# Two-layer decoder step: reordered loads, stores and waits at four seams, one test around the overflow loop, last-stage gathers two tiles ahead

## The chip, the core and the metric

The kernel runs on one core of one Trainium2 chip, as one launch. The metric is the device time of the launch in microseconds (us). Five engines run their own instruction streams and meet at semaphores: PE (matrix multiplication; its weight loads are listed as PEld), DVE (vector), ACT (activation functions; it also issues DMAs), POOL (indirect DMAs, the gathers) and SP (only issues DMAs and waits). A DMA issued by an engine stands in that engine's queue; the packets of all queues run on the same 16 DMA engines of the core.

## The reference

One step of a two-layer decoder on 1024 prompt rows and 8 sample rows, all in float32, width 1024. Each layer projects its input, runs three groups of heads (a gated convolution, latent attention, an mLSTM), multiplies with `w_out`, and sends each row to two of 32 experts. Cut to what bears on the change:

```python
def hybrid_layer(x, p, pos, ...):
    z = jnp.einsum('bld,dn->bln', x, w_in)
    q = jnp.einsum('blr,rn->bln', rms_norm(c_q, q_norm_g), w_uq)...
    ckv = rms_norm(c_kv, kv_norm_g)
    att = mla_prompt_attention(q_nope, q_rope, k_nope, krope, v)
    h_m, C1, n1, m1 = mlstm_chunkwise(...)
    y = rms_norm(jnp.concatenate([y_conv, y_mla, y_mlstm], -1)..., mix_norm_g)
    h1 = layer_norm(DN_ALPHA * x + jnp.einsum('blm,md->bld', y, w_out), ln1_g, ln1_b)
    moe = hier_moe(h1, ...)
    ple = jnp.einsum('blp,pd->bld', p, w_pe) * jax.nn.sigmoid(jnp.einsum('bld,de->ble', h1, w_pg))
    out = layer_norm(DN_ALPHA * h1 + moe + ple, ln2_g, ln2_b)
    return out, ckv, krope, conv_state, C1, n1, m1
```

## The kernel before

**Tiles and stages.** The rows are nine tiles: eight of 128 prompt rows (`TP` = 8) and a last one with the 8 sample rows (`LAST` = `TP`, `NT` = 9). A layer is four stages: `stream_project_prepare` (projections, mLSTM, queries, keys, values), prompt attention, sample attention, and `mix_route_experts` (`w_out`, routing, the gates `sigmoid(h1 @ w_pg)`, the experts). After layer 1 `combine_last` adds the expert rows to the base and normalises. Each engine's instructions of a stage are written out by hand in one function; waits are semaphore counts, so an engine that waits holds up all that stands behind it on that engine. Between stages every engine waits at a barrier (L114, one for each run of semaphores). The expert stage's loads follow a planned list of due times per expert.

**Projection to attention.** On SP, round `t` of the projection stores what tile `t-1` gave: latents (L408, L409), KT, V, QT (L433), then Y, the mLSTM output (L438, behind `y_ready`); in the round `t == LAST` the samples' Z follows (L441). The round `t == NT` loads the first pair of heads for attention (`first_qk`, L218 and L219, four loads of 96x1024; `first_v`, L227) and stores the sample tile's latents and its QT (96x8x8). SP then waits at L449 for the QT stores, which ends the stage on SP. The attention's first matmul is L1149.

**Gates.** `EARLY` lists the tiles whose gates are made before the experts start; the sample tile is number 4 of them. For number `i` ACT takes the sigmoid of PE's product (L2474, L2487 for the samples) into `sig[i % 2]`, copies a transposed p tile out of PSUM for PE (`p_copied`, L2459, which also issues the load of a later p tile, L2429), and stores the finished base rows of number `i-1` (`stored_base`, L2470). `sig` has two buffers, so from `i` = 2 on a wait for the store of number `i-2` stands ahead. The p tiles alternate between early and deferred ones (`P_ORDER`); deferred gates are made between the expert quads. PE transposes p (L2187) and multiplies it with `w_pe` (L2130, L2236).

**Overflow loop.** 21 quads of experts run with fixed capacity. Rows that don't fit go to at most 32 further blocks; their count `used` is read on the device and SP, PE, ACT and DVE each run `rest_turns` over them. Here `used` is 0.

**Last stage.** SP loads nine `base` tiles and the rows `g`, `b` of 128x1024; POOL gathers two expert rows per token into `r1`, `r2` (two indirect DMAs a tile, L2945); PE adds, for each tile, `ident @ base` (L2956) and `diag(weight) @ r` (L2960) in one PSUM tile; ACT builds the 18 diagonals (L3007); DVE and ACT normalise, SP stores the output.

## Time and profile before

| | |
|---|---|
| device time, median of 3 runs | 2455.68 us (2449.44 to 2460.41) |
| the profiled execution | 2454.07 us, of which the span of its instructions is 2452.3 us |
| PE busy | 2246.9 us, 92% of the span |
| DVE, ACT, POOL busy | 1160.3, 729.4, 335.6 us |
| HBM traffic | 382.90 MB read, 126.32 MB written, 208 GB/s over the span |

### The profile page before, as it was taken

The page shows a single profiled execution, that of the slowest core. Times are in us where ns is not written, and L with a number is a line of the kernel's source. Part 1 is how long each engine was busy: PE and PEld are TensorE (multiplying, and loading weights), DVE is VectorE, ACT ScalarE, POOL GpSimd, SP SyncE. Part 2 cuts the span into 40 slices and gives each one's busy share as a digit, 9 for nine tenths or more (in the row PEclk, how much of TensorE's full clock was granted, in tenths as well). Part 3 has the DMA queues.
Part 4 walks back from the last instruction along what each step waited for, and adds up shares of the span by engine and source line. Part 5 has one row for each costly group of instructions (what it writes and reads, how often), then busy time and mean ns, then how long its engine had stood idle before and what let it go on. Part 6 is the DMA issues. An engine that isn't in the chain of part 4 may idle for free. (4 is left out here: it accounts for less than half of the span.)

```text
span 2452.3 us, 39565 instructions
## 1 busy us (share of the span) xinstructions
PE 2246.9 (92%) x14448; PEld 1164.2 (47%) x14448; DVE 1160.3 (47%) x2954; ACT 729.4 (30%) x1454; POOL 335.6 (14%) x514
## 2 busy tenths in 40 slices
PE   7999987989999999999599999688889999999977
PEld 3555554557455443333255555455655544333323
DVE  3444444665686312322345554466568752222226
ACT  2555553543211011000145545444323011110012
POOL 1021006830000200000100000296000020000011
PEclk9999998998999999999799999899899999999998
DMA  9476127733510869999753421565323146899976
GB/s 342 161 261 237 59 60 191 198 71 122 193 56 5 347 238 363 406 420 420 260 186 94 129 69 51 151 191 146 122 73 147 31 188 256 343 374 421 420 299 248
DMA packets 229654, 512.00 MB, mean 209 GB/s; under 512 B 60614, under 2 KB 138382, under 8 KB 204088
## 3 DMA queue, kind: packets, MB, share of 16 engines
q1 hardware_dynamic: 182760, 385.68, 43.6%
q0 software_dynamic: 27136, 85.62, 9.8%
q10 hardware_dynamic: 19552, 38.02, 4.2%
q8 instruction: 121, 1.98, 0.3%
q14 instruction: 85, 0.70, 0.1%
HBM read 382.90 MB, written 126.32 MB: 208 GB/s over the span
## 5 line engine op out<-in xcount | busy, mean ns | idle before, releaser
L507 PE MATMUL pj_zp<-pj_w,pj_xT 128*128 128x512 f32 (+1 forms) x1280 | 504.5, 541 | 5.9 <-DMA pj_w<-in_w_in 5.9
L507 PEld LDWEIGHTS pj_zp<-pj_w,pj_xT 128*128 128x128 f32 x1280 | 225.5, 192 | 204.4 <-issue 193.0
L2325 PE MATMUL op_bank<-ex_wgu,h 128*32 128x512 f32 x2688 | 297.1, 594 | 3.2 <-DMA ex_wgu<-in_e_up 3.2
L2148 PE MATMUL op_bank<-op_wout,op_hT 128*128 128x512 f32 x512 | 226.9, 601 | 3.1 <-DVE h L2632 1.7
L2869 DVE TENSOR_TENSOR ex_h<-ex_sil,op_bank 128x256 f32<-128x256 f32 x42 | 17.7, 421 | 367.1 <-ACT ex_sil L2513 367.1
L2325 PEld LDWEIGHTS op_bank<-ex_wgu,h 128*32 128x32 f32 x2688 | 84.5, 110 | 190.6 <-issue 187.4
L2345 PE MATMUL op_bank<-ex_wd,ex_hT 128*32 128x512 f32 x1344 | 154.6, 601 | 8.9 <-DMA ex_wd<-in_e_down 7.4
L2148 PEld LDWEIGHTS op_bank<-op_wout,op_hT 128*128 128x128 f32 x512 | 97.4, 193 | 120.7 <-issue 118.4
L1248 ACT ACTIVATE at_p<-at_s,at_nmx 128x640 f32<-128x640 f32 (+7 forms) x128 | 94.8, 740 | 172.7 <-DVE at_nmx L1211 172.1
L2513 ACT ACTIVATE ex_sil<-op_bank 128x256 f32<-128x256 f32 x42 | 16.1, 383 | 423.7 <-PE op_bank L2325 423.7
L1159 PE MATMUL at_tp<-ident,at_p 128*128 128x128 f32 x576 | 88.3, 281 | 35.8 <-DVE at_pT L1217 25.2
L2220 PE MATMUL op_bank<-op_wpg,op_hT 128*128 128x512 f32 x256 | 115.6, 606 | 0.0
L2111 POOL DMA_INDIRECT scratch_XR<-h,route_row x36 | 36.6, 1018 | 523.8 <-DVEq L2839 513.4
L1209 DVE TENSOR_REDUCE at_mx<-at_s 128x1 f32<-128x640 f32 (+7 forms) x128 | 97.0, 758 | 4.5
L1149 PE MATMUL at_s<-first_qk 96*128 96x512 f32 (+3 forms) x192 | 78.2, 523 | 21.1 <-PEq L114 21.1
L950 ACT ACTIVATE pj_z<-pj_zp 128x512 f32<-128x512 f32 (+1 forms) x80 | 43.2, 540 | 176.3 <-PE pj_zp L507 176.3
L1159 PEld LDWEIGHTS at_tp<-ident,at_p 128*128 128x128 f32 x576 | 62.5, 141 | 65.8 <-issue 60.5
L478 POOL DMA_INDIRECT pj_r<-scratch_YR,route_row x18 | 18.9, 1052 | 540.9 <-issue 357.5
L1207 DVE TENSOR_TENSOR at_s<-at_s,at_mask 128x128 f32<-128x128 f32 x128 | 38.3, 300 | 103.0 <-PE at_s L1149 101.1
L2246 PE MATMUL op_bank<-op_wpg,op_hT 128*128 128x512 f32 x192 | 84.4, 593 | 0.0
L2345 PEld LDWEIGHTS op_bank<-ex_wd,ex_hT 128*32 128x32 f32 x1344 | 40.9, 110 | 91.0 <-issue 84.8
L2220 PEld LDWEIGHTS op_bank<-op_wpg,op_hT 128*128 128x128 f32 x256 | 49.4, 196 | 59.9 <-issue 59.7
(486 smaller groups left out, 3453.2 us busy)
## 6 DMA issues: line engine op xcount, KB each, us to landing
ex_wgu<-in_e_gate SPq DMA_DIRECT2D x64, 1024.0 KB, 11.6
ex_wgu<-in_e_up SPq DMA_DIRECT2D x64, 1024.0 KB, 15.0
ex_wd<-in_e_down SPq DMA_DIRECT2D x64, 1024.0 KB, 18.0
h<-scratch_XR SPq DMA_DIRECT2D x42, 512.0 KB, 16.9
scratch_XR<-pj_zero POOLq DMA_DIRECT2D x38, 512.0 KB, 7.8
pj_w<-in_w_in SPq DMA_DIRECT2D x8, 2048.0 KB, 17.9
pc_ckv<-in_cache_ckv SPq DMA_DIRECT2D x200, 64.0 KB, 2.0
cv_cch<-scratch_Z POOLq DMA_DIRECT2D x48, 256.0 KB, 4.3
```

The costliest lines, as they stand in the source:

```text
L507: last = pe.matmul(zp[c % ZB][:, 0:cn], xT[:, t % 2, k, :], w[:, k, c0:c0 + cn], start=(k == 0), stop=(k == KC - 1), skip_group_check=True)
L950: act.activation(z[:, t % 2, c0:c0 + cn], zp[c % ZB][:, 0:cn], ACT.Copy).then_inc(z_ready, 1)
L1149: last = pe.matmul(scores_of(n)[:, c:min(c + 512, width)], queries(j, s)[:, qb * P:(qb + 1) * P], keys(j, s)[:, c:min(c + 512, width)], st ...
L1159: last = pe.transpose(tp[e][:, kb % 4, :], probs[small(n)][units[n][1]][:, kb, :], ident[:, :])
L1207: st.did(dve.tensor_tensor(diag, diag, mask[:, :], ALU.add))
L1209: st.did(dve.tensor_reduce(mx[:, k:k + 1], out[:, 0:(qb + 1) * P], AX.X, ALU.max))
L1248: act.activation(probs[small(n)][s][:, 0:qb + 1, :].rearrange("p b n -> p (b n)"), scores_of(n)[:, 0:(qb + 1) * P], ACT.Exp, bias=nmx[:, k ...
L2148: last = pe.matmul(op[n][:, :], hT[:, t, c, :], wout[:, c, n * 512:(n + 1) * 512], start=(c == 0), stop=(c == KC - 1))
L2220: last = pe.matmul(gpair[i % 2][n][:, :], hT[:, t, c, :], wpg[:, c, n * 512:(n + 1) * 512], start=(c == 0), stop=(c == KC - 1))
L2246: last = pe.matmul(dbank[:, :], hT[:, DEFERRED[j], c, :], wpg[:, c, n * 512:(n + 1) * 512], start=(c == 0), stop=(c == KC - 1))
L2325: last = pe.matmul(gu[q % 2][part], xT[q % 2][:, c, part], wgu[s][:, :, c, :], start=(c == 0), stop=(c == KC - 1), skip_group_check=True)
L2345: last = pe.matmul(yp[n][part, :], heT[:, q % 2, c, part], wd[s][:, c, n * 512:(n + 1) * 512], start=(c == 0), stop=(c == 1), skip_group_c ...
```

## The change

1. Projection to attention, both layers, SP: in the round `t == LAST` the sample tile's latents and the loads of the first pair are issued right behind the QT store of tile 7, ahead of the wait for the last Y. The sample tile's QT store leaves SP's queue and becomes ACT's last instruction of the stage (semaphore `q_last`).
2. Gates, both layers, ACT: for the sample tile the two `p_copied` and the `stored_base(3)` come first, the wait for the base store and the sigmoid last.
3. Overflow loop, four engines: a loop of 2 turns with a test and 16 tested copies of the body becomes one test of `used > 0` around a loop of 32 turns with one tested body.
4. Last stage: on SP `base` tiles 0 and 1 come first, then `g` and `b`, and `base` tile `t` waits until the gathers of tile `t-2` have landed; the gathers of tile `t` wait for the same on POOL. PE adds the base of tiles 0 and 1 first and from then on the base of tile `t+2` behind the gathered rows of tile `t`; it waits for the two diagonals of a tile only, not for all 18.

The hunk that declares the semaphore `q_last` is left out:

```diff
--- before.py
+++ after.py
@@ -355,6 +356,24 @@
                 def load_w(n):
                     c0, cn = Z_CHUNKS[n]
                     sp.dma_start(w[:, :, c0:c0 + cn], of_layer(d["w_in"], layer).rearrange("(p k) n -> p k n", k=KC)[:, :, c0:c0 + cn]).then_inc(w_loaded[n], 16)
+
+                def latents_stored(u, n):
+                    sp.wait_ge(lat_ready, u + 1)
+                    sp.dma_start(of_layer(d["ckv_all"], layer)[rows(u, n)], ckvn[0:n, :]).then_inc(c_stored, 16)
+                    sp.dma_start(of_layer(d["krope_all"], layer)[rows(u, n)], kpad[0:n, NOPE:]).then_inc(c_stored, 16)
+
+                def first_pair_loaded():
+                    sp.wait_ge(k_stored, 16 * TP)
+                    sp.wait_ge(q_stored, 16 * TP)
+                    sp.wait_ge(normed, NT)
+                    first.load_qk(sp, d, 0)
+                    sp.wait_ge(turned, 2 * NT)
+                    for s in range(2):
+                        sp.wait_ge(y_kept[s], 16 * len(range(s, NT, 2)))
+                    first.load_qk(sp, d, 1)
+                    sp.wait_ge(v_stored, 16 * TP)
+                    sp.wait_ge(o_ready, NT)
+                    first.load_v(sp, d)
 
                 def keep(t):
                     sp.wait_ge(o_ready, t + 1)
@@ -386,27 +405,12 @@
                     sp.dma_start(dst, src).then_inc(ml_loaded, 16)
                 sp.dma_start(cache.table[:, :], d["page_table"]).then_inc(cache.table_loaded, 16)
                 sp.wait_ge(cache.table_loaded, 16)
-                for t in range(NT + 1):
+                for t in range(NT):
                     u = t - 1
                     if t + 3 < NT:
                         load(t + 3)
-                    if t == NT:
-                        sp.wait_ge(k_stored, 16 * TP)
-                        sp.wait_ge(q_stored, 16 * TP)
-                        sp.wait_ge(normed, NT)
-                        first.load_qk(sp, d, 0)
-                        sp.wait_ge(turned, 2 * NT)
-                        for s in range(2):
-                            sp.wait_ge(y_kept[s], 16 * len(range(s, NT, 2)))
-                        first.load_qk(sp, d, 1)
-                        sp.wait_ge(v_stored, 16 * TP)
-                        sp.wait_ge(o_ready, NT)
-                        first.load_v(sp, d)
-                    if is_tile(u):
-                        n = P if u < LAST else DECB
-                        sp.wait_ge(lat_ready, u + 1)
-                        sp.dma_start(of_layer(d["ckv_all"], layer)[rows(u, n)], ckvn[0:n, :]).then_inc(c_stored, 16)
-                        sp.dma_start(of_layer(d["krope_all"], layer)[rows(u, n)], kpad[0:n, NOPE:]).then_inc(c_stored, 16)
+                    if is_chunk(u):
+                        latents_stored(u, P)
                     if t < TP:
                         sp.wait_ge(z_ready, NZ * t + 2)
                         sp.dma_start(d["Z"][ds(PAD + t * P, P), 0:C_Q], z[:, t % 2, 0:C_Q]).then_inc(z_stored[t % 2], 16)
@@ -427,12 +431,14 @@
                         sp.dma_start(d["KT"][:, :, rows(u)].rearrange("h p n -> p h n"), kT[:, :, :]).then_inc(k_stored, 16)
                         sp.wait_ge(v_out, u + 1)
                         sp.dma_start(d["V"][rows(u)], v[:, :]).then_inc(v_stored, 16)
-                    if is_tile(u):
-                        n = P if u < LAST else DECB
+                    if is_chunk(u):
                         sp.wait_ge(qT_out, 2 * u + 2)
-                        sp.dma_start(d["QT"][:, :, rows(u, n)].rearrange("h p n -> p h n"), qT[:, :, 0:n]).then_inc(q_stored, 16)
+                        sp.dma_start(d["QT"][:, :, rows(u)].rearrange("h p n -> p h n"), qT[:, :, :]).then_inc(q_stored, 16)
                     if t + 2 < NT:
                         keep(t + 2)
+                    if t == LAST:
+                        latents_stored(LAST, DECB)
+                        first_pair_loaded()
                     if is_chunk(u):
                         sp.wait_ge(y_ready, u + 1)
                         sp.dma_start(d["Y"][rows(u), CONVW + H * VD:], y[:, :]).then_inc(y_stored, 16)
@@ -442,7 +448,8 @@
                 sp.wait_ge(c_stored, 32 * NT)
                 sp.wait_ge(k_stored, 16 * TP)
                 sp.wait_ge(v_stored, 16 * TP)
-                sp.wait_ge(q_stored, 16 * NT)
+                sp.wait_ge(q_stored, 16 * TP)
+                sp.wait_ge(q_last, 16)
                 sp.wait_ge(y_stored, 16 * TP)
                 for s in range(2):
                     sp.wait_ge(y_kept[s], 16 * len(range(s, NT, 2)))
@@ -1047,6 +1054,8 @@
                             act.wait_ge(y_ready, u)
                         act.activation(so[:, :], z[:, u % 2, C_MO:C_MO + MW], ACT.Sigmoid).then_inc(so_ready, 1)
                     projected_out(t, 4)
+                act.wait_ge(qT_out, 2 * NT)
+                act.dma_start(d["QT"][:, :, rows(LAST, DECB)].rearrange("h p n -> p h n"), qT[:, :, 0:DECB]).then_inc(q_last, 16)
 
 
 
@@ -1821,7 +1830,6 @@
 EARLY, DEFERRED = (0, 1, 2, 3, TP, 4), (5, 6, 7)
 HALVES = 2 * len(DEFERRED)
 LEAD = 2
-REST_STEP = 16
 P_ORDER = ((0, 0), (1, 0), (2, 0), (3, 0), (0, 1), (4, 0), (1, 1), (5, 0), (2, 1))
 
 
@@ -1855,11 +1863,10 @@
 
 def rest_turns(eng, used):
 
-    with eng.Fori(0, -(-BLOCKS // REST_STEP)) as r:
-        with eng.If(REST_STEP * r < used):
-            for i in range(REST_STEP):
-                with eng.If(REST_STEP * r + i < used):
-                    yield REST_STEP * r + i
+    with eng.If(used > 0):
+        with eng.Fori(0, BLOCKS) as b:
+            with eng.If(b < used):
+                yield b
 
 
 def mix_route_experts(nc, d, layer, ident, step, out):
@@ -2474,17 +2481,20 @@
                     act.activation(sig[:, i % 2, n * 512:(n + 1) * 512], gpair[i % 2][n][:, :], ACT.Sigmoid).then_inc(sig_done, 1)
 
                 for i, t in enumerate(EARLY):
+                    if t == TP:
+                        p_copied(P_ORDER.index((i, 0)))
+                        p_copied(P_ORDER.index((i - 3, 1)))
+                        stored_base(i - 1)
+                        act.wait_ge(base_stored[i % 2], 16 * (i // 2))
+                        act.wait_ge(g_done, 2 * i + 2)
+                        act.activation(sig[:, i % 2, 0:SCOLS], gpair[i % 2][0][:, 0:SCOLS], ACT.Sigmoid).then_inc(sig_done, 2)
+                        continue
                     if i >= 2:
                         act.wait_ge(base_stored[i % 2], 16 * (i // 2))
-                    if t < TP:
-                        sigmoid(i, 0)
+                    sigmoid(i, 0)
                     if i >= 2:
                         p_copied(P_ORDER.index((i, 0)))
-                    if t < TP:
-                        sigmoid(i, 1)
-                    else:
-                        act.wait_ge(g_done, 2 * i + 2)
-                        act.activation(sig[:, i % 2, 0:SCOLS], gpair[i % 2][0][:, 0:SCOLS], ACT.Sigmoid).then_inc(sig_done, 2)
+                    sigmoid(i, 1)
                     if i >= 3:
                         p_copied(P_ORDER.index((i - 3, 1)))
                     if i:
@@ -2924,10 +2934,12 @@
             @block.sync
             def _(sp):
                 for t in range(NT):
-                    sp.dma_start(base[:, t, :], d["BASE"][rows(t)]).then_inc(loaded[t], 16)
-                    if t == 0:
+                    if t >= 2:
+                        sp.wait_ge(gathered[t - 2], 32)
+                    if t == 2:
                         for buf, which in ((g, "ln2_g"), (b, "ln2_b")):
                             sp.dma_start(buf[:, :], row_of_layer(d[which], layer)).then_inc(gains, 16)
+                    sp.dma_start(base[:, t, :], d["BASE"][rows(t)]).then_inc(loaded[t], 16)
                 for t in range(NT):
                     sp.wait_ge(o_ready, t + 1)
                     sp.dma_start(d["y_all"][rows(t)], o[:, t % 4, :]).then_inc(stored[t % 4], 16)
@@ -2939,6 +2951,8 @@
                 pool.wait_ge(d["sw"]["last_rows"], 16 * LAYERS)
                 for t in range(NT):
                     m = P if t < TP else DECB
+                    if t >= 2:
+                        pool.wait_ge(gathered[t - 2], 32)
                     if t == TP:
                         pool.wait_ge(zeroed, 2)
                     for k, r in ((0, r1), (1, r2)):
@@ -2947,19 +2961,28 @@
 
             @block.tensor
             def _(pe):
-                pe.wait_ge(diag_ready, 2 * NT)
-                for t in range(NT):
+                def bases(t):
                     pe.wait_ge(loaded[t], 16)
                     if t >= 4:
                         pe.wait_ge(scaled, t - 3)
                     for n in range(2):
                         pe.matmul(acc[t % 4][:, n * 512:(n + 1) * 512], ident[:, :], base[:, t, n * 512:(n + 1) * 512], start=True, stop=False)
+
+                def gathered_rows(t):
+                    pe.wait_ge(diag_ready, 2 * t + 2)
                     pe.wait_ge(gathered[t], 32)
                     for n in range(2):
                         for k, r in ((0, r1), (1, r2)):
                             last = pe.matmul(acc[t % 4][:, n * 512:(n + 1) * 512], diag[:, k, t, :], r[:, t, n * 512:(n + 1) * 512],
                                              start=False, stop=(k == 1))
                         last.then_inc(summed, 1)
+
+                bases(0)
+                bases(1)
+                for t in range(NT):
+                    gathered_rows(t)
+                    if t + 2 < NT:
+                        bases(t + 2)
 
             @block.vector
             def _(dve):
```

Where it moves instructions. SP at the end of the projection in layer 0, before (names are destination <- source):

```order
L433 DMA scratch_QT<-mp_qT 96x8x128
L438 DMA scratch_Y<-ml_y 128x256
L441 DMA scratch_Z<-pj_z 8x2216
L218 DMA first_qk<-scratch_QT 96x1024
L219 DMA first_qk<-scratch_KT 96x1024
L218 DMA first_qk<-scratch_QT 96x1024
L219 DMA first_qk<-scratch_KT 96x1024
L227 DMA first_v<-scratch_V 128x8x128
L408 DMA out_ckv_all<-mp_ckvn 8x128
L409 DMA out_krope_all<-mp_kpad 8x32
L433 DMA scratch_QT<-mp_qT 96x8x8
```

and after:

```order
L436 DMA scratch_QT<-mp_qT 96x8x128
L362 DMA out_ckv_all<-mp_ckvn 8x128
L363 DMA out_krope_all<-mp_kpad 8x32
L218 DMA first_qk<-scratch_QT 96x1024
L219 DMA first_qk<-scratch_KT 96x1024
L218 DMA first_qk<-scratch_QT 96x1024
L219 DMA first_qk<-scratch_KT 96x1024
L227 DMA first_v<-scratch_V 128x8x128
L444 DMA scratch_Y<-ml_y 128x256
L447 DMA scratch_Z<-pj_z 8x2216
```

The first pair now stands ahead of Y (`ml_y`) and Z (`pj_z`), and the small QT store is gone from SP.

ACT in the gates of layer 0, from the sigmoid of number 3 on, before (`ms_C` is here the buffer of the deferred p tile):

```order
L2474 ACTIVATE op_sig<-op_bank 128x512
L2429 DMA op_p<-in_p_all 128x256
L2459 ACTIVATE ms_C<-op_bank 128x256
L2470 DMA scratch_BASE<-op_sig 128x1024
L2429 DMA op_p<-in_p_all 128x256
L2459 ACTIVATE op_pT<-op_bank 128x256
L2487 ACTIVATE op_sig<-op_bank 128x256
L2429 DMA op_p<-in_p_all 128x256
L2459 ACTIVATE ms_C<-op_bank 128x256
L2470 DMA scratch_BASE<-op_sig 128x1024
L2474 ACTIVATE op_sig<-op_bank 128x512
```

and after:

```order
L2481 ACTIVATE op_sig<-op_bank 128x512
L2436 DMA op_p<-in_p_all 128x256
L2466 ACTIVATE ms_C<-op_bank 128x256
L2477 DMA scratch_BASE<-op_sig 128x1024
L2436 DMA op_p<-in_p_all 128x256
L2466 ACTIVATE op_pT<-op_bank 128x256
L2436 DMA op_p<-in_p_all 128x256
L2466 ACTIVATE ms_C<-op_bank 128x256
L2477 DMA scratch_BASE<-op_sig 128x1024
L2490 ACTIVATE op_sig<-op_bank 128x256
L2481 ACTIVATE op_sig<-op_bank 128x512
```

The sigmoid of 128x256, behind whose wait for the base store the other rows stood, is now behind both p copies and the next base store.

SP in the last stage, before:

```order
L2927 DMA fi_base<-scratch_BASE 128x1024
L2930 DMA fi_g<-in_ln_g 128x1024
L2930 DMA fi_b<-in_ln_b 128x1024
L2927 DMA fi_base<-scratch_BASE 128x1024 x8
L2933 DMA out_y_all<-fi_o 128x1024 x9
```

and after:

```order
L2942 DMA fi_base<-scratch_BASE 128x1024 x2
L2941 DMA fi_g<-in_ln_g 128x1024
L2941 DMA fi_b<-in_ln_b 128x1024
L2942 DMA fi_base<-scratch_BASE 128x1024 x7
L2945 DMA out_y_all<-fi_o 128x1024 x9
```

`g` and `b` move behind the second base tile; what the rows can't show is that the last seven base loads now each wait for gathers.

## Rows read from the trace of the kernel before

**Rows 1.** Page, part 1: busy us (share of the span) and instructions.
```profile
PE 2246.9 (92%) x14448; PEld 1164.2 (47%) x14448; DVE 1160.3 (47%) x2954; ACT 729.4 (30%) x1454; POOL 335.6 (14%) x514
```

**Rows 2.** Timeline of SP, layer 0's seam: start us, us, line, operation.
```profile
358.39 0.32 SPq L433 DMA_DIRECT2D scratch_QT<-mp_qT  x1
364.89 0.32 SPq L438 DMA_DIRECT2D scratch_Y<-ml_y  x1
...
367.88 0.39 SPq L227 DMA_DIRECT2D first_v<-scratch_V  x1
...
369.70 0.33 SPq L433 DMA_DIRECT2D scratch_QT<-mp_qT  x1
```

**Rows 3.** Windows at both seams: stretch us, engines' busy us, PEclk, DMA share, GB/s.
```profile
361.30:364.80 3.50, 2.40 (x8) 1.48 (x9) 3.15 (x10) 0.49 (x1) 0.00 (x0) 1.00 0.00 0
366.20:376.40 10.20, 1.08 (x8) 0.83 (x8) 1.39 (x7) 1.08 (x2) 0.00 (x0) 0.71 0.95 211
368.36:378.69 10.33, 0.00 (x1) 0.03 (x1) 0.00 (x0) 0.78 (x3) 0.00 (x0) 0.61 0.80 169
1558.94:1569.74 10.80, 0.00 (x1) 0.03 (x1) 0.00 (x0) 0.77 (x3) 0.00 (x0) 0.63 0.72 162
```

**Rows 4.** Line L449, SP's last waits: durations ns min/median/max.
```profile
L449 SPq EVENT_SEMAPHORE  x4: 28/3416/7048, 370.1 to 1567.6; - x4
```

**Rows 5.** Timeline of ACT in layer 0's gates: [idle before <-releaser].
```profile
835.80 1.24 ACTq L2470 DMA_DIRECT2D scratch_BASE<-op_sig  x1
...
844.93 0.38 ACT L2459 ACTIVATE op_pT<-op_bank 128x256 f32<-128x256 f32 x1 [8.78 <-DMA scratch_BASE<-op_sig]
```

**Rows 6.** Windows at the same places: PE's idle stretches, then the low clock.
```profile
842.61:845.46 2.85, 0.00 (x0) 0.03 (x1) 0.00 (x0) 0.53 (x2) 0.00 (x0) 0.92 0.38 131
844.99:851.82 6.83, 6.36 (x23) 2.74 (x24) 3.48 (x6) 0.98 (x3) 0.00 (x0) 0.50 0.90 260
2035.34:2038.94 3.60, 0.00 (x0) 0.03 (x1) 0.00 (x0) 0.53 (x2) 0.00 (x0) 1.00 0.30 110
2039.65:2043.07 3.42, 3.42 (x19) 1.37 (x12) 1.74 (x5) 0.38 (x1) 0.00 (x0) 0.50 0.93 344
```

**Rows 7.** Window over the second half of layer 0's expert quads.
```profile
1007.00:1165.00 158.00, 156.13 (x1370) 55.09 (x1366) 43.35 (x78) 4.98 (x13) 0.00 (x0) 1.00 1.02 420
```

**Rows 8.** Line L1859, the test inside the overflow loop: ns min/median/max.
```profile
L1859 PEldq COMPARE_BRANCH  x4: 221/1905/5080, 1176.9 to 2374.6; - x4
```

**Rows 9.** Line L2002, the end of the block that holds the loop.
```profile
L2002 ACTq DRAIN  x2: 8/8/8, 1182.1 to 2375.7; - x2
...
L2002 PEldq DRAIN  x2: 8/8/8, 1183.1 to 2375.1; - x2
...
L2002 DVEq DRAIN  x2: 17/17/17, 1183.3 to 2374.6; - x2
```

**Rows 10.** Timeline of PE in the last stage.
```profile
2384.76 3.48 PE L2956 MATMUL fi_acc<-fi_base,ident 128*128 128x512 f32 x4 [11.96 <-ACT fi_diag L3007]
2392.04 6.67 PE L2960 MATMUL fi_acc<-fi_r,fi_diag 128*128 128x512 f32 x8 [3.79 <-DMA fi_r<-scratch_YR,route_row]
...
2400.26 3.60 PE L2960 MATMUL fi_acc<-fi_r,fi_diag 128*128 128x512 f32 x8
...
2436.31 3.60 PE L2960 MATMUL fi_acc<-fi_r,fi_diag 128*128 128x512 f32 x8
```

**Rows 11.** Line L2945, gathers of the last stage: ns, first and last start us.
```profile
L2945 POOL DMA_INDIRECT fi_r<-scratch_YR,route_row x18: 933/1011/1075, 2380.1 to 2402.5; - x18
...
DMA to landing us min/median/max: 9.3/17.7/20.3
```

**Rows 12.** Line L478, the same gathers in layer 1's first stage.
```profile
DMA to landing us min/median/max: 4.2/7.3/9.0
```

**Rows 13.** Line L2927, the loads of base in the last stage.
```profile
DMA to landing us min/median/max: 3.7/15.6/22.5
```

**Rows 14.** Line L2930, the loads of g and b.
```profile
DMA to landing us min/median/max: 5.0/5.7/6.5
```

More of the change, by code:

```diff
@@ L325, in stream_project_prepare @@
             ph.sem(n) for n in ("q_done", "q_out", "k_done", "k_out", "v_done", "v_out", "r_steps", "rope_out", "qt_done", "qT_out"))
-        c_stored, k_stored, v_stored, q_stored, y_stored = (ph.sem(n) for n in ("c_stored", "k_stored", "v_stored", "q_stored", "y_stored"))
+        c_stored, k_stored, v_stored, q_stored, y_stored, q_last = (
+            ph.sem(n) for n in ("c_stored", "k_stored", "v_stored", "q_stored", "y_stored", "q_last"))
         qk_done, qk_out, g_steps, g_neg, g_exp, g_sum, g_ln, gate_ready, gate_done, gate_out = (
```

## The prediction

> **What bounds the kernel now.** The page first: PE is busy 92% of the span [rows 1], so what can be won is where PE stands still, and where it works at its low clock behind a standstill. So I read, in each of the four places that the diff touches, PE's idle stretch and its releaser in the timeline, then the queue of the engine that releases it, then the granted clock in windows over that place. All sums are made against the profiled execution (2454.07 us, 1.8 us of it outside the span), which lies 1.6 us under the median of before; that is added at the end.
>
> **Projection to attention.** SP issues the QT store of tile 7 at 358.39 and nothing more before Y at 364.89; the first pair follows, its last load (V) at 367.88, and the samples' QT at 369.70 [rows 2]. The DMA engines move nothing from 361.30 to 364.80 and are then 95% busy until 376.40 [rows 3]. SP's wait at L449 starts at 370.1 and lasts 7.05 [rows 4], to 377.2; the barrier follows, and PE has stood from 368.36 to 378.69; in layer 1 from 1558.94 to 1569.74 [rows 3]. So this seam is bounded by a burst of about 10 us of packets that could start some 4 us sooner.
>
> The change puts the pair right behind QT. Its waits are for stores issued until 358.39, whose packets are through when the queues fall idle at 361.30, so I put its first load at 361.7; V was issued 3.0 after Y, by which the first load was near 365.7. The gain at the head is 4.0. The two latent stores now go ahead of it; they hide in the wait for QT 7. Y and Z are ready by 364.89 and now wait behind the pair's packets: 128 KB and 71 KB by their shapes, about 1 us at the 211 GB/s of this burst, an estimate. ACT issues QT near 369.7 on its own queue; nothing is queued behind it on ACT. I take half a microsecond off the 4.0 for these and get 3.6 a layer. Bounds: PE's last work ends at 368.36 and QT cannot leave before 369.7; with 2 us to land, SP ends at 371.7, a gain of 5.5. If QT's packets, which have only 32 bytes, come last and slowly, the burst ends only 1 us sooner. The clock already falls within the standstill (0.61 and 0.63 on its mean, [rows 3]), so a shorter one keeps the cold start behind it; I count nothing for it. **Two layers: 7.2 (2 to 11).**
>
> **Gates.** ACT issues the base store at 835.80 and next copies p at 844.93, after 8.78 us of waiting for that store [rows 5]. PE has run out at 842.61 and stands 2.85 us; from 844.99 to 851.82 it is granted 0.50, with 6.36 us of work that would take 3.2 at full clock. In layer 1 it stands 3.60, then 3.42 us at 0.50, half of which is lost [rows 6]. With the p copies ahead of the wait, both copies can follow PE's transposes at once; what still waits for the store is the samples' sigmoid, which no matmul needs before the next sigmoids. The losses are 2.85 + 3.2 and 3.60 + 1.7, 11.3 in all. What is late next is the deferred p tile, whose load ACT issues just ahead of that base store: I leave 1.0 for it. The next base store goes out sooner as well, so the following sigmoid does not wait longer than now. **10.3 (6 to 11.3).** It passes on only if the experts follow. They do as long as their loads are triggered by PE freeing slots; against it speaks the second half of the quads, where the DMA engines are full (share 1.02, 420 GB/s) while PE is busy 156.13 of 158.00 us [rows 7]. That stretch is bound by both; but its loads too start when PE frees a slot, so it shifts as a whole.
>
> **Overflow loop.** With `used` = 0 nothing is computed; the cost is branches at the end of the stage. PE's test at L1859 took 5.08 us at 1176.9; of four executions, two a layer, the shortest took 0.22 and the median is 1.905, so layer 1's long one was near 3.6 [rows 8]. The block ends when the last engine drains: in layer 0 DVE at 1183.3, PE at 1183.1, ACT at 1182.1; in layer 1 ACT at 2375.7, PE at 2375.1, DVE at 2374.6 [rows 9]. Two turns become one test, which saves all engines their second turn, some 1 us. Were the long branch gone as well, PE would be through near 1178 and ACT would decide. I take 1.5 in layer 0 and 1.0 in layer 1. **2.5 (0.8 to 3.5).** The barriers behind it stay, in number and kind.
>
> PE's 5.08 us branch has a rule: the Trainium skill, "Runtime: NRT & Kernel Launch", Instruction fetch mechanics, says that a taken branch whose target is outside the two pages that the engine holds must fetch before going on. The rows agree that PE's jump over the unrolled copies is slow, 5.08 against 0.22. By that rule the jump over the one body that is left may be as slow; PE would then still end near its old drain, and the part would give the lower bound, 0.8, the sum 2435.4.
>
> **Last stage.** PE starts at 2384.76, when the last diagonal is done, at low clock (four base matmuls in 3.48), then stands 3.79 us for the first gathers and does the first rows in 6.67 instead of 3.60 [rows 10]. From 2400.26 to 2436.31 it runs 7 tiles in 36.05, 5.15 a tile; behind PE's last tile some 12.4 us of normalising and storing follow, which the change leaves. After: base 0 needs 3.7 to land [rows 13], so PE starts near 2383 and has two bases done by 2388. The first gathers are issued at the same time as before with less beside them. The gathers of layer 1's first stage landed in 7.3 [rows 12]; 18 of them start within 22.4 us here, 1.3 apart [rows 11], so tile 0 lands near 2388. PE does its rows until 2391.5 and then wants base 2. That is new: base 2 is issued only when tile 0 has landed, and `g` and `b` are ahead of it, which took 5.0 and 6.5 [rows 14]. By the longer, with some 0.7 for issuing, it lands near 2395.2. PE stands 3.7 us, which all three standstills of that size in these rows answered with the low clock; so I take 3.4 lost there too, as for the window of 6.83 us [rows 6]. Then 7 bases and 8 tiles of rows remain, 39.5 us by the matmul durations above (1.72 and 3.43): PE ends at 2438.1 against 2439.9. **2 (0 if the stall is longer by 2, 8.9 if base 2 comes in time).** The new waits hold only base loads on SP and gathers on POOL, and on SP the output stores behind the last base load, which four output buffers cover.
>
> **Sum.** 7.2 + 10.3 + 2.5 + 2 = 22.0, so 2432.1 for an execution like the profiled one, 2433.7 against the median: I say 2433.
>
> **Rivals.** (1) The expert stage takes back the gates' gain, since its DMA engines are full: then 2433 + 10.3 = 2443. For it speaks the share of 1.02 in rows 7; against it that PE hardly waits there.
>
> (2) The seam's wait only moves. The pair's burst is the same length, Y, Z and QT now lie behind or in it, and L449 waits for all of them. With 1 us a layer the time is 2438. For it: 95% busy DMA engines; against: 3.5 idle us ahead of the burst. This is where the Trainium skill speaks against the change: "DMA: Bandwidth & Descriptors", Issuing engines are not separate DMA queues, says that transfers issued by several engines interleave on the same 16 engines and that a second issuer saves only issue time. By that rule QT on ACT's queue gives nothing; my 3.6 does not rest on it but on the earlier issue.
>
> (3) Slower: the gathers become the bound. Tile `t` is issued only when `t-2` has landed, so a pair of tiles costs one landing time R from first issue to last landing. Tiles 0, 2, 4, 6, 8 land at 2388 + R, 2R, 3R, 4R. PE reaches tile 8 at about 2434.7, so it is hidden up to R = 11.6; layer 1's 7.3 to 9.0 and the 1.3 between two issues give 8.6 to 10.3 [rows 12]. But the gathers of this stage took 9.3 to 20.3, median 17.7 [rows 11]. At 17.7 tile 8's rows start at 2458.8 instead of 2436.31, a loss of 22.5 that eats the other 20.0: 2458. At 20.3 it is 2469.2, a loss of 32.9: 2469. From R = 17.1 on the kernel is slower. Against it: those times were taken with 18 gathers and nine base loads issued at once, the new order has at most four gathers and about two bases in flight.
>
> **Chances.** The forecast with its parts inside their bounds 0.68; rival 1 0.10; rival 2 0.12; rival 3 0.06 (half of it with a small loss only); anything else 0.04. The forecast's own range is 2423 to 2439. Rivals 1 and 2 reach to 2443, so the range is 2421 to 2443. Half a per cent, 12.3 us, is about what a measurement of this kernel can tell from no change: faster means under 2443.4. The forecast and rival 2 lie there, rival 1 on the edge: faster 0.85, same 0.12, slower 0.03.
>
> **What would show it.** Right: the pair's loads issued near 361.7 and L449's wait ending 3 to 4 us sooner; no idle of PE ahead of L2187 at the gates and no low clock behind it, with the first quad 10 us earlier over both layers; PE's test at the loop once a layer; in the last stage PE standing between the first and the second tile's rows, ahead of a base matmul, then 5.15 us a tile. Wrong: DMA packets of the pair still running at 376; PE waiting for expert weights in sum 5 us more than now; PE idle ahead of L2976 (the gathered rows) in the later tiles.

## The result and the profile after

The changed kernel takes 2430.09 us in the median of 4 runs (2428.36 to 2431.01), before in the same comparison 2457.61; the ratio is 0.9892, 95% interval 0.9873 to 0.9911. A second timing of it, at the end of the experiments, gave 2431.12. The span of the profiled execution is 2429.3 us against 2452.3, so 23.0 us are to be found in the trace. The table cuts both traces at the same instructions: first matmul with `w_in` in the projections, first of attention, first of the gates, first of the experts' gate-and-up, end of the last expert matmul, first base load on SP, end of PE's last matmul, end of the span. Every length is the difference of two starts (or ends) in the timeline; the last column is after less before.

| stretch | before us | after us | change |
|---|---|---|---|
| projections to attention, layer 0 | 361.51 | 358.63 | -2.89 |
| gates, layer 0 | 118.79 | 112.91 | -5.88 |
| experts, layer 0 | 303.73 | 305.07 | +1.34 |
| last expert matmul to layer 1's projections | 29.25 | 26.43 | -2.82 |
| projections to attention, layer 1 | 361.34 | 359.16 | -2.17 |
| gates, layer 1 | 118.29 | 112.99 | -5.30 |
| experts, layer 1 | 305.22 | 304.73 | -0.50 |
| last expert matmul to first base load | 6.53 | 4.43 | -2.09 |
| last stage, first base load to end | 72.98 | 72.54 | -0.43 |
| all others together | | | -2.3 |

SP's timeline at the seam of layer 0, after, answers to [rows 2]:

```profile
358.48 0.32 SPq L436 DMA_DIRECT2D scratch_QT<-mp_qT  x1
...
362.41 0.32 SPq L218 DMA_DIRECT2D first_qk<-scratch_QT  x1
...
364.50 0.39 SPq L227 DMA_DIRECT2D first_v<-scratch_V  x1
365.03 0.64 SPq L444 DMA_DIRECT2D scratch_Y<-ml_y  x1
```

The pair starts at 362.41 and its last load at 364.50, 3.4 us ahead of before; Y is now behind it. The windows over the pair's burst and over PE's standstill, after, answer to [rows 3]:

```profile
362.40:372.80 10.40, 4.36 (x20) 2.76 (x20) 4.08 (x16) 2.06 (x4) 0.00 (x0) 0.91 0.92 224
368.51:375.41 6.90, 0.00 (x0) 0.03 (x1) 0.00 (x0) 0.77 (x3) 0.00 (x0) 0.67 0.65 140
```

The burst has the same length and the same share of the DMA engines, only sooner, and PE stands 6.90 us instead of 10.33. In the waits of layer 1's seam the longest of PE is 7.2 instead of 10.80.

PE's timeline at the gates of layer 0, after, and the granted clock in windows there in both layers, answer to [rows 6]:

```profile
838.75 0.51 PE L2194 MATMUL op_bank<-ident,op_p 128*128 128x128 f32 x2
839.19 1.07 PE L2137 MATMUL op_bank<-op_wpe,op_pT 128*32 128x256 f32 x16
840.19 7.13 PE L2227 MATMUL op_bank<-op_wpg,op_hT 128*128 128x512 f32 x16
```

```profile
838.80:845.60 6.80, 6.80 (x35) 3.23 (x32) 3.58 (x6) 0.77 (x2) 0.00 (x0) 1.00 0.84 292
2020.58:2027.40 6.82, 6.82 (x35) 3.25 (x32) 2.88 (x6) 0.77 (x2) 0.00 (x0) 1.00 0.83 297
```

No idle time stands ahead of these transposes of the p tile (L2194), PE is busy all of either window, and the clock stays at full (PEclk 1.00). The 16 gate matmuls from 840.19 take 7.13.

The test of the overflow loop on PE, after, answers to [rows 8]: two executions, none long.

```profile
L1866 PEldq COMPARE_BRANCH  x2: 212/290/367, 1168.2 to 2349.7; - x2
```

The stage is over when the last engine has drained. These rows answer to [rows 9]:

```profile
L2009 PEldq DRAIN  x2: 2252/2330/2407, 1168.7 to 2350.0; - x2
L2009 DVEq DRAIN  x2: 423/424/425, 1171.2 to 2352.7; - x2
L2009 ACTq DRAIN  x2: 8/8/8, 1172.5 to 2354.0; - x2
```

ACT is now the last in both layers; before, it was DVE in layer 0 and ACT in layer 1, and PE, whose test took longest, in neither.

PE's timeline in the last stage, after, with ACT's waits in it, answers to [rows 10]:

```profile
2360.44 5.57 PE L2969 MATMUL fi_acc<-fi_base,ident 128*128 128x512 f32 x8 [8.12 <-DMA fi_base<-scratch_BASE]
2365.85 3.60 PE L2976 MATMUL fi_acc<-fi_r,fi_diag 128*128 128x512 f32 x8
2374.78 3.51 PE L2969 MATMUL fi_acc<-fi_base,ident 128*128 128x512 f32 x4 [5.34 <-DMA fi_base<-scratch_BASE]
2378.13 3.60 PE L2976 MATMUL fi_acc<-fi_r,fi_diag 128*128 128x512 f32 x8
...
2409.03 7.03 PE L2976 MATMUL fi_acc<-fi_r,fi_diag 128*128 128x512 f32 x16
```

```profile
2374.78:2378.13 3.35, 3.35 (x5) 1.52 (x5) 0.00 (x0) 0.00 (x0) 0.00 (x0) 0.54 0.93 378
```

```profile
ACT fi_o L3038 <- DMA out_y_all<-fi_o: 4.9, 1, 4.9
```

The standstill has moved from the first gathers to base 2 and grown to 5.34 us; the base matmuls behind it are slow (3.51 against 1.88, at a granted clock of 0.54). The last two tiles' rows lie back to back (x16), and ACT waits once for an output store, 4.9 us, which the prediction did not have.

### The profile page after: what moved, and what is told of

The parts are those of the page before. It is cut to its first block and busy times, and to the rows that moved or that the text cites. A ratio compares the mean times of both kernels' runs of the same rounds, so it can differ in the third digit from the quotient of the medians.

```text
span 2429.3 us, 39510 instructions
## 1 busy us (share of the span) xinstructions
PE 2243.3 (92%) x14448; PEld 1161.9 (48%) x14448; DVE 1160.2 (48%) x2954; ACT 729.7 (30%) x1454; POOL 336.6 (14%) x514
## 5 line engine op out<-in xcount | busy, mean ns | idle before, releaser
L2879 DVE TENSOR_TENSOR ex_h<-ex_sil,op_bank 128x256 f32<-128x256 f32 x42 | 17.7, 421 | 369.4 <-ACT ex_sil L2523 369.4
L1158 PE MATMUL at_s<-first_qk 96*128 96x512 f32 (+3 forms) x192 | 78.1, 522 | 14.1 <-PEq L114 14.1
```

Source lines behind the costliest of these rows:

```text
L1158: last = pe.matmul(scores_of(n)[:, c:min(c + 512, width)], queries(j, s)[:, qb * P:(qb + 1) * P], keys(j, s)[:, c:min(c + 512, width)], st ...
```

## The experiments

The first four put one part of the change into the kernel before; the other parts stay as they were.

**The seam alone.** Core of the edit:

```diff
-                    if t == NT:
-                        sp.wait_ge(k_stored, 16 * TP)
...
+                    if t == LAST:
+                        latents_stored(LAST, DECB)
+                        first_pair_loaded()
...
+                act.dma_start(d["QT"][:, :, rows(LAST, DECB)].rearrange("h p n -> p h n"), qT[:, :, 0:DECB]).then_inc(q_last, 16)
```

> The kernel before with the seam between projection and attention alone reordered (SP and ACT, both layers). Theory: the parts add up, each in its own stage; the changed kernel shortened the stretch from the first projection matmul to the first attention matmul by 2.9 us in layer 0 and 2.2 in layer 1, and PE's standstill there from 10.33 to 6.90, so here the time falls by 5 to 7 us. Rival: the wait only moves and the gain came from elsewhere; then less than 2 us.

Measured: ratio 0.9953 (0.993 to 0.9976), medians 2447.86 and 2457.39. In the trace the two stretches to attention shorten by 3.70 and 2.73 us, 6.4 in all, and PE's standstills are 6.8 and 6.4. The gain is in the stretches where it was expected, and the rival falls. The timed gain, 9.5 us between the medians and 6 to 17 by the ratio, is larger than the 5 to 7 expected.

**The gates alone.**

```diff
+                    if t == TP:
+                        p_copied(P_ORDER.index((i, 0)))
+                        p_copied(P_ORDER.index((i - 3, 1)))
+                        stored_base(i - 1)
+                        act.wait_ge(base_stored[i % 2], 16 * (i // 2))
```

> The kernel before with ACT's order in the gates alone changed. Theory: the gate stretch shortens by 5.9 us in layer 0 and 5.3 in layer 1, as in the changed kernel, and the expert quads behind it shift as a whole, so the time falls by 10 to 12 us. Rival: the experts' full DMA engines take part of it back; then the expert stretch grows by 3 us or more a layer and the time falls by 6 us or less.

Measured: 0.9947 (0.9924 to 0.9969), 2445.08. The gate stretches shorten by 5.90 and 4.89 us, 10.8 in all; the expert stretches change by +1.18 and -0.32. They also vary by up to 3 us in kernels that leave the gates alone (+3.01 in layer 0 with the loop alone, +2.28 with the last stage alone), so nothing of the gain is seen to be taken back. The rival falls.

**The loop alone.**

```diff
-    with eng.Fori(0, -(-BLOCKS // REST_STEP)) as r:
-        with eng.If(REST_STEP * r < used):
-            for i in range(REST_STEP):
-                with eng.If(REST_STEP * r + i < used):
-                    yield REST_STEP * r + i
+    with eng.If(used > 0):
+        with eng.Fori(0, BLOCKS) as b:
+            with eng.If(b < used):
+                yield b
```

> The kernel before with the overflow loop alone changed. Theory: the stretch from the last expert matmul to the first work of the next stage shortens by 2.8 us in layer 0 and 2.1 in layer 1, the time by 4 to 5 us, since PE's long branch (5.08 us) becomes one of 0.2 to 0.4 us. Rival: that stretch shortened because other parts shifted the stores in it; then 2 us or less.

Measured: 0.9953 (0.9936 to 0.9971), 2447.40, that is 7 to 16 us by the ratio and 10.0 between the medians. The two stretches behind the experts shorten by 2.71 and 2.09, 4.8 in all, as expected, and the rival falls. The timed gain is larger than the traced one and than the 4 to 5 expected; the next kernel shows one possible reason.

**The last stage alone.**

```diff
+                    if t >= 2:
+                        sp.wait_ge(gathered[t - 2], 32)
-                    if t == 0:
+                    if t == 2:
...
+                bases(0)
+                bases(1)
+                for t in range(NT):
+                    gathered_rows(t)
+                    if t + 2 < NT:
+                        bases(t + 2)
```

> The kernel before with the last stage alone changed. Theory: PE's standstill moves from the first gathers (3.8 us) to the third base tile (5.3 us) and the stage as a whole keeps its length; the time changes by less than 1 us. Rival: the stage gains the forecast 2 us or more, and the changed kernel lost it only by its earlier start; then 2 to 3 us less.

Measured: 0.9982 (0.9967 to 0.9996), 2455.57. From the first base load to the end the stage is 0.7 us longer than in the kernel before (PE starts 1.72 sooner; PE's part, from its first base matmul to its last matmul, is 1.56 longer; the end, from there to the end of the span, is 0.87 longer). So the stage gains nothing, and the rival falls. The ratio is a little under 1 all the same; what gives that is not seen. This kernel still has the old loop, and in its profile the stretch behind layer 0's experts is 6.15 us longer than in the kernel before. The test on PE there:

```profile
L1859 PEldq COMPARE_BRANCH  x4: 233/3822/8027, 1177.0 to 2378.6; - x4
```

Of its four executions one took 8.03 us (before: 5.08 at most), and PE, which drains at 1190.1, is the last engine there. So the old jump has no fixed price, and a single profile can miss some of it.

The four parts do not add up in the timing. By the ratios they are worth 11.5, 13.0, 11.5 and 4.4 us, 40 together, where the whole change gives 26.5; in the traces they are worth 6.4, 10.8, 4.8 and -0.7, that is 21.3 of the 23.0. All four were timed against the same 19 runs of the kernel before, which lie between 2452.19 and 2465.72, so the size of a part is better read from the traces.

**The copies put back inside the one test** (on the changed kernel).

```diff
-        with eng.Fori(0, BLOCKS) as b:
-            with eng.If(b < used):
-                yield b
+        with eng.Fori(0, BLOCKS // 16) as r:
+            for i in range(16):
+                with eng.If(16 * r + i < used):
+                    yield 16 * r + i
```

> The changed kernel with sixteen unrolled copies of the overflow body, in a loop of two turns, inside the one test of used > 0. Theory: what cost time was jumping over the sixteen copies, on PE 3.9 to 8.0 us a jump in two of the kernels with the old loop; PE's one taken jump now lasts 3 us or more again in layer 0 and the stretch behind the last expert matmul grows by 0.5 to 2 us there. Rival: the two turns with their inner tests cost the time, not the length of the jump; then PE's jump stays under 0.5 us and the stretch stays as in the changed kernel.

```profile
L1866 PEldq COMPARE_BRANCH  x2: 3341/3531/3721, 1169.9 to 2352.2; - x2
L1866 DVEq COMPARE_BRANCH  x2: 72/74/76, 1172.6 to 2354.9; - x2
...
L2010 PEldq DRAIN  x2: 8/8/8, 1173.7 to 2355.6; - x2
L2010 ACTq DRAIN  x2: 8/8/8, 1174.5 to 2356.7; - x2
L2010 DVEq DRAIN  x2: 52/76/99, 1175.5 to 2355.5; - x2
```

Measured: 2435.31 in one run. The jump on PE takes 3.3 and 3.7 us, against 0.21 and 0.37 with one body, at the same test and with the same number of turns run (none); the two stretches behind the experts grow by 1.26 and 1.05. So it is the length of the code that is jumped, not the number of tests, and the rival falls. But PE is not the engine that ends the stage, as the theory has it. In layer 0 that is DVE: its test takes 0.08 us at 1172.6, but its drain comes only at 1175.5, behind those of PE and ACT. With one body the test is at 1171.0 and the drain at 1171.2. In layer 1 ACT is last with sixteen copies as with one, 0.3 us later behind the last expert matmul; the rest of the 1.05 comes behind the drains, where 3.5 us pass until the first base load instead of 2.7. What makes the barriers longer there is not shown.

**QT back on SP's queue** (on the changed kernel).

```diff
+                sp.wait_ge(qT_out, 2 * NT)
+                sp.dma_start(d["QT"][:, :, rows(LAST, DECB)].rearrange("h p n -> p h n"), qT[:, :, 0:DECB]).then_inc(q_last, 16)
                 sp.wait_ge(c_stored, 32 * NT)
...
-                act.wait_ge(qT_out, 2 * NT)
-                act.dma_start(d["QT"][:, :, rows(LAST, DECB)].rearrange("h p n -> p h n"), qT[:, :, 0:DECB]).then_inc(q_last, 16)
```

> The changed kernel with the sample tile's QT store back on SP's queue, as its last store behind Y and Z. Theory: transfers of one queue go in order, so its 32-byte packets now start only behind V's and Z's, and the last store lands 1 to 2 us later; PE's standstill at the seam grows from 6.9 to 8 us or more in each layer. Rival, by the rule of the Trainium skill (DMA: Bandwidth & Descriptors, Issuing engines are not separate DMA queues): only issue time is saved by the second issuer; the standstill stays within 0.5 us.

PE's wait ahead of attention, in layer 0 and in layer 1:

```profile
PE at_s L1158 <- PEq L114: 6.0, 1, 6.0
...
PE at_s L1158 <- PEq L114: 8.0, 1, 8.0
```

Measured: 2430.51 in one run. 6.0 and 8.0 add up to 14.0, with QT on ACT's queue 6.9 and 7.2 to 14.1. My theory of 1 us or more a layer falls; in sum the runs agree with the rule that the rival names, though each layer lies 0.8 to 0.9 from its counterpart, more than the rival gave it. In the nine traces with QT on ACT's queue the standstill scatters as widely, 6.4 to 7.4 in layer 0 and 6.4 to 8.6 in layer 1, so one run cannot show half a microsecond.

**g and b behind base 2** (on the changed kernel).

```diff
                     if t >= 2:
                         sp.wait_ge(gathered[t - 2], 32)
+                    sp.dma_start(base[:, t, :], d["BASE"][rows(t)]).then_inc(loaded[t], 16)
                     if t == 2:
                         for buf, which in ((g, "ln2_g"), (b, "ln2_b")):
                             sp.dma_start(buf[:, :], row_of_layer(d[which], layer)).then_inc(gains, 16)
-                    sp.dma_start(base[:, t, :], d["BASE"][rows(t)]).then_inc(loaded[t], 16)
```

> The changed kernel with g and b issued behind base tile 2 instead of ahead of it; all waits stay. Theory: base 2 came 5.3 us late because g and b lie ahead of it on SP's queue; now it lands some 4 us sooner, PE's standstill behind the first rows falls from 5.3 to under 2 us, and the last stage shortens by 3 to 7 us. Rival: base 2 is late because it is issued only when tile 0 has landed, in the middle of the gathers of tiles 1 and 2; then the standstill stays above 4 us.

```profile
2363.71 3.60 PE L2976 MATMUL fi_acc<-fi_r,fi_diag 128*128 128x512 f32 x8
2367.43 1.98 PE L2969 MATMUL fi_acc<-fi_base,ident 128*128 128x512 f32 x4
...
2374.82 3.02 PE L2969 MATMUL fi_acc<-fi_base,ident 128*128 128x512 f32 x4 [1.98 <-DMA fi_base<-scratch_BASE]
```

```profile
ACT fi_o L3038 <- DMA out_y_all<-fi_o: 8.4, 1, 8.4
```

Measured: 2429.22 in one run. Base 2 is there in time, the standstill at its place is gone; 1.98 us stand ahead of base 3. PE's part is 1.79 us shorter, but the stage as a whole 0.2 longer: what PE won came back behind it, where ACT now waits 8.4 us for an output store and the end (from PE's last matmul on) is 15.25 us long instead of 13.23. The theory is right on the standstill and wrong on the stage.

**Three base tiles ahead** (on the changed kernel).

```diff
-                    if t >= 2:
-                        sp.wait_ge(gathered[t - 2], 32)
-                    if t == 2:
+                    if t >= 3:
+                        sp.wait_ge(gathered[t - 3], 32)
+                    if t == 3:
```

> The changed kernel with three base tiles issued at once and base t waiting for the gathers of tile t-3; g and b stand ahead of base 3. Theory (g and b ahead of base 2 cost the standstill): base 2 is there in time, the first gathers land 1 to 2 us later, the wait moves partly to base 3; the last stage shortens by 2 to 5 us. Rival (the burst of 0.5 MB transfers at the start is what costs, in whatever order): PE's standstills up to tile 3 still add up to 5 us or more and the stage keeps its length.

Measured: 2430.28 in one run. PE's standstills up to tile 3 are 0.40, 0.44 and 1.00 us, so the rival falls. PE's part is 3.85 us shorter, the end again 15.24 long, with a wait of 8.1 on the same store; the stage wins 1.8, a little less than the 2 to 5 expected.

**POOL's wait taken out** (on the changed kernel).

```diff
-                    if t >= 2:
-                        pool.wait_ge(gathered[t - 2], 32)
```

> The changed kernel with POOL's wait between gathers taken out: all 18 gathers are issued at once as before the change, base loads still follow the gathers. Theory: the wait keeps room for the first tiles and for base 2; without it the packets of later gathers crowd base 2, which lands later than 9.7 us behind the first gathers, and PE stands 8 us or more; the stage grows by 2 us or more. Rival: the wait is what makes base 2 and the later rows late; then the stage shortens.

```profile
2375.76 3.58 PE L2967 MATMUL fi_acc<-fi_base,ident 128*128 128x512 f32 x4 [8.44 <-DMA fi_base<-scratch_BASE]
```

Its gathers (with POOL's wait: median 6.7):

```profile
DMA to landing us min/median/max: 6.1/11.7/17.0
```

Measured: 2432.06 in one run. PE stands 8.44 us for base 2 and the stage is 2.9 us longer, as the theory has it. So holding the gathers back makes the bases land sooner, which is the opposite of rival 3 of the prediction.

**Four output stores between the base loads** (on the changed kernel; `store_o` is the wait for `o_ready` and the store).

```diff
                     sp.dma_start(base[:, t, :], d["BASE"][rows(t)]).then_inc(loaded[t], 16)
-                for t in range(NT):
+                    if t >= 5:
+                        store_o(t - 5)
+                for t in range(NT - 5, NT):
+                    store_o(t)
```

> The changed kernel with the first four output stores issued between the base loads 5 to 8 instead of behind all of them. Theory: ACT stood 4.9 us for output buffer 0, whose store lay behind base load 8 on SP; that wait goes, and the stretch from PE's last matmul to the end falls from 13.2 to at most 12.4 us, PE's own part unchanged. Rival: the longer end comes from PE's last two tiles lying back to back; then it stays above 13 us although ACT does not wait.

Measured: 2428.54 in one run. ACT's waits after 2395 no longer hold a DMA, but the end is still 13.22 us long. The rival is right: in the changed kernel the 0.85 us of the longer end come with PE's last two tiles back to back (16 matmuls at once, behind which DVE has two tiles left to do), not with the store. ACT's last two rows in the changed kernel give the size:

```profile
2416.49 1.20 ACT L3038 ACTIVATE fi_o<-fi_acc,fi_shift,fi_rs 128x1024 f32<-128x1024 f32 x1 [2.46 <-DVE fi_shift L3008]
...
2420.79 1.20 ACT L3038 ACTIVATE fi_o<-fi_acc,fi_shift,fi_rs 128x1024 f32<-128x1024 f32 x1 [2.46 <-DVE fi_shift L3008]
```

DVE and ACT take 4.30 us for a tile, and PE's last tile comes 3.43 us behind the one before it (7.03 less 3.60), which leaves 0.87.

**Three base tiles ahead and four stores between, together** (on the changed kernel; the two edits are those above).

> The changed kernel with three base tiles ahead (g and b ahead of base 3) and the first four output stores between the base loads. Theory: both losses of the last stage are gone: PE's part falls from 55.6 to some 52 us, the end from 13.2 to under 13, so the kernel is 4 to 5 us faster than the changed one, 2425 to 2426. Rival: the stores between hold up base loads 6 to 8 and the gathers; then PE stands for a later base tile and less than 2 us is won.

```profile
2359.59 5.38 PE L2974 MATMUL fi_acc<-fi_base,ident 128*128 128x512 f32 x8 [8.12 <-DMA fi_base<-scratch_BASE]
2364.81 3.63 PE L2981 MATMUL fi_acc<-fi_r,fi_diag 128*128 128x512 f32 x8
2368.28 1.88 PE L2974 MATMUL fi_acc<-fi_base,ident 128*128 128x512 f32 x4
...
2373.43 1.92 PE L2974 MATMUL fi_acc<-fi_base,ident 128*128 128x512 f32 x4
...
2403.39 7.03 PE L2981 MATMUL fi_acc<-fi_r,fi_diag 128*128 128x512 f32 x16
```

Measured: 0.9882 (0.9861 to 0.9903), median 2428.65 of 6 runs (2425.34 to 2430.68). PE runs from base 0 on without a standstill over 0.83 us, its part is 50.84 us instead of 55.62, the end 13.23: the stage is 4.8 us shorter, and the rival falls. The end was expected under 13 and the time at 2425 to 2426; neither came out so. With three ahead alone the end was 15.24, so here the stores between are worth the 2 us that they were not worth above.

**The changed kernel again.**

> The changed kernel once more, unaltered, to have its spread beside that of the version with three base tiles ahead and stores between. Theory: the last stage is as long as in its first profile, 72.5 us, against 67.8 with that version, and the median is 2429 to 2431, some 2 to 5 us above that version's 2428.7 or better. Rival: the 4.8 us of the last stage drown in what varies elsewhere from run to run; then both medians lie within 1 us.

Measured: 0.9898 (0.988 to 0.9916), median 2431.12 of 6 runs (2429.82 to 2432.19); last stage 71.98 us. The version with both edits, timed on another chip, lies 2.5 us lower, but the two intervals overlap: its 4.8 us are shown in the trace of the stage, not settled by the timing.

## Why the prediction was right, and where it was not

The forecast of 2433 was 3 us too high, and its 22.0 us compare with 23.0 between the two spans. That the sum comes so close is in part luck. The seam and the last stage gave 3.7 less than forecast, the gates and the loop 3.3 more; the experts' stretches grew by 0.8, and 2.3 of the 23.0 lie in stretches that the change does not touch.

Two terms held. **The seam**: 7.2 forecast; PE's two standstills fell by 3.4 and 3.6, 7.0, and the stretches by 5.1, or 6.4 with this part alone. These stretches scatter by some 3 us from trace to trace; between the means of the four traces with the old order and the ten with the new one lie 8.0. The pair started at 362.41, not at 361.7, since SP waits for the QT store of tile 7 to land (2.1 us in layer 0) and not only for its packets. **The gates**: 10.3 forecast, 11.2 found, 10.8 with this part alone; the whole of 11.3 that was lost there came back, and the 1.0 left for the p load was not needed. It reached the end because the experts' stretch did not grow by more than it varies. **Rival 2** had its store of QT right (a second queue gives nothing that is seen, 14.0 against 14.1 us of standstill) and its conclusion wrong: it is the earlier issue that counts, as the forecast said.

The step that failed in size most is the next. **The overflow loop**: 2.5 forecast, with 3.5 as the upper bound; 4.9 found, 4.8 alone. In layer 0 (1.5 forecast, 2.8 found) I looked at PE's long jump and gave DVE, the last to drain there [rows 9], no more than its second turn. But DVE too goes on late behind a jump over sixteen copies, 2.8 us as the kernel with the copies put back shows; with one body that is gone, and ACT ends the stage. In layer 1 (1.0 forecast, 2.1 found) ACT was last before and after, and its second turn was worth 1.2, about as forecast (its drain comes 2.9 us behind the last expert matmul before, 1.7 after). The other 0.9 come from the barriers, which "stay, in number and kind" but not in time: from ACT's drain to the first base load 3.6 us passed before and 2.7 after. PE's own jump, 0.21 to 0.37 us with one body, ended the stage in neither layer of the profiled execution. Its price goes with the length of the code passed: long jumps of 3.3 to 8.0 us over sixteen copies, none over one, though over sixteen not every jump is long (0.22 at least, [rows 8]). The rule of the Trainium skill (Runtime: NRT & Kernel Launch, Instruction fetch mechanics) makes this depend on whether the target is still held. The runs agree with that for one body against sixteen; why a second turn took 8.03 once they do not show. The 0.8 that I drew from the rule, with one body as slow as sixteen, was wrong.

**The last stage** was mis-sized too: 2 forecast, 0.4 found, 0.7 lost with the part alone. In the five traces that have the new order of this stage unaltered it lasts 71.98 to 73.68 us, in the four with the old one 72.71 to 73.21, so no gain is seen. The mechanism was the one forecast, a standstill for base 2 behind `g` and `b` and the low clock behind it; base 2 landed 8.8 us after its issue instead of the 6.5 of [rows 14], so PE stood 5.34 instead of 3.7. The low clock then cost 1.6 (one group of 3.51 instead of 1.88) and not the 3.4 forecast, so the two errors cancel by luck: PE's part took 55.6 us, 55.1 by the forecast. The step that failed there is the sentence on the 12.4 us behind PE's last tile, "which the change leaves": the end took 13.23, since PE's last two tiles now lie back to back, and these 0.85 were not in the sum at all. The sentence that the output stores "four output buffers cover" was wrong as well: the store of tile 0 waits on SP for base 8, thus for the gathers of tile 6, and ACT stood 4.9 us for its buffer. In the changed kernel that is hidden, since without it the end is as long (13.22); it would have cost 2 us as soon as PE was faster, as the kernel with three tiles ahead shows.

Rival 3 did not come true, but its condition was not far. The gathers landed in 6.0 to 10.4 us, median 6.7, against 17.7 of [rows 11]:

```profile
DMA to landing us min/median/max: 6.0/6.7/10.4
```

Its R, the time that a pair of tiles costs, was 10.1 in the mean from the first gather's issue at 2357.57 to tile 8's at 2397.97, where the prediction had worked out 8.6 to 10.3 and called it hidden up to 11.6. The longest was 12.5:

```profile
2365.82 1.01 POOL L2959 DMA_INDIRECT fi_r<-scratch_YR,route_row  x1 [3.20 <-DMA fi_r<-scratch_YR,route_row]
...
2378.28 1.01 POOL L2959 DMA_INDIRECT fi_r<-scratch_YR,route_row  x1 [7.51 <-DMA fi_r<-scratch_YR,route_row]
```

In the version with both edits, where PE is faster, it does stand for later gathers, 0.83 us at most.

What stays open: why the loop alone gives 7 to 16 us in the timing where its trace gives 4.8, and why the barriers of layer 1 take less time without the copies. The jump that took 8.03 in one kernel is a part of the first at most; how often it does so in unprofiled runs was not measured.

## What to carry to other kernels

When a wait on an issuing queue guards one transfer, look for others behind it that don't need it, and move them ahead; the gain here was the idle time of the DMA engines in front (3.5 us, of which PE won 3.4), whichever queue the small store went by. When loads are made to wait for consumers, list what else stands behind them on that queue: here the output stores, which cost nothing until the matmuls became faster. A loop that runs zero times still costs its jump on every engine that has it, and in this kernel the jump grew with the code it had to pass; look for the engine that drains last, which need not be the one with the longest test.

## What was not expected of the hardware

PE's first jump over sixteen copies of the body took 3.3 to 5.1 us and once, in a second turn, 8.03; over one copy 0.21 to 0.37. DVE's test took 0.08 us in either case, but over sixteen copies its next instruction came up to 2.8 us later, which the row of the test itself does not show. Gathers issued at most four at a time landed in a median of 6.7 us, all at once in 11.7 (one run, the base loads held back as before it) and in 17.7 in the kernel before, where nine base loads were issued beside them. Holding them back made the whole stage 2.9 us shorter than letting them go.
